# Bisection rounds 18 to 20 without prompt heads, the roots of the recurrence one round later, products without use on TensorE

## The reference, cut to what matters

```python
idx, valid = select_topk(indexer_scores(qi, wi, ki_all), q_pos, k_pos, topk)   # sample tokens: 256 of 4097
p = jax.nn.softmax(jnp.where(valid, logits + bias, -jnp.inf)); out = p @ v     # prompt: 8 heads, 4 blocks of 128 queries
u = jnp.sqrt(-jnp.expm1(2.0 * log_a)) * (i * xc)                               # recurrence, 512 channels
hs = scan(h = a * h + u)
```

## Time and profile before

| | us |
|---|---|
| median of the runs | 1295.65 |
| the profiled execution's own time | 1298.16 |
| its span, first to last instruction | 1296.4 |
| the stretch of the rounds in it | 210.0 to 283.4 |
| busy: PE, DVE, ACT, POOL | 1259.2, 696.9, 464.3, 186.4 |
| mean granted clock of PE | 0.986 |

### The profile page before, as it was taken

The page is one execution under the profiler, slowest core; times in us unless marked ns, Lnnn a source line. Parts: engine busy times, 40 slices in busy tenths (PEclk is TensorE's granted clock), DMA queues, the critical chain, the costliest instruction groups (busy, mean ns, idle before and its releaser), DMA issues.

```text
span 1296.4 us, 24716 instructions
## 1 busy us (share of the span) xinstructions
PE 1259.2 (97%) x10122; PEld 1219.1 (94%) x10122; DVE 696.9 (54%) x1292; ACT 464.3 (36%) x538; POOL 186.4 (14%) x281
## 2 busy tenths in 40 slices
PE   5999998899999999999999999999999999999997
PEld 5979995678999999999999999999999999999996
DVE  5468887677265555555323355547655555542222
ACT  5242326652153434334222244334433334331110
POOL 1101002135041111111000010034111111110000
PEclk9999989899999999999999999999999999999997
DMA  6653302023032222222222231222222222222211
GB/s 221 167 123 136 125 34 80 1 78 122 1 136 98 70 92 97 97 97 85 87 98 92 106 130 66 73 92 68 96 97 97 97 83 79 97 89 91 90 63 66
DMA packets 26595, 120.40 MB, mean 93 GB/s; under 512 B 7880, under 2 KB 9224, under 8 KB 14504
## 3 DMA queue, kind: packets, MB, share of 16 engines
q1 hardware_dynamic: 21784, 107.67, 24.4%
q0 software_dynamic: 2048, 10.54, 2.4%
q10 hardware_dynamic: 2704, 1.35, 0.4%
HBM read 115.94 MB, written 3.61 MB: 92 GB/s over the span
## 4 chain that ended last, share of the span: by engine, by line
PE 70%; DVE 2%; ACT 0%; issue 0%; DVEq 0%
PE ps L881 22%; PE ps L880 22%; PE ps L883 22%; PE ps L1016 1%; PE ps L1013 1%; PE ps L1014 1%; PE ps L899 1%; PE ps L1367 1%; DVE vtc L2028 0%; DVE yt L2075 0%; PE ps L1384 0%; DVE xn L1424 0%; PE ps L1397 0%; PE ps L1357 0%; DVE w_l L1410 0%; DVE ut L2021 0%
## 5 line engine op out<-in xcount | busy, mean ns | idle before, releaser
L880 PE MATMUL ps<-xh,w_h 128*128 128x260 f32 x1664 | 435.6, 283 | 0.2
L881 PE MATMUL ps<-xl,w_h 128*128 128x260 f32 x1664 | 434.7, 283 | 0.0
L883 PE MATMUL ps<-xh,w_l 128*128 128x260 f32 x1664 | 334.6, 283 | 0.0
L880 PEld LDWEIGHTS ps<-xh,w_h 128*128 128x128 f32 x1664 | 313.9, 189 | 0.7 <-DVE res L1829 0.3
L881 PEld LDWEIGHTS ps<-xl,w_h 128*128 128x128 f32 x1664 | 313.5, 188 | 0.1
L1410 DVE TENSOR_TENSOR w_l<-w_raw,w_h 128x2048 fp32r<-128x2048 f32 (+1 forms) x94 | 213.1, 2267 | 158.8 <-ACT w_h L526 158.6
L883 PEld LDWEIGHTS ps<-xh,w_l 128*128 128x128 f32 x1664 | 256.3, 188 | 0.0
L526 ACT ACTIVATE w_h<-w_raw 128x2048 fp32r<-128x2048 f32 (+1 forms) x50 | 92.3, 1846 | 256.4 <-PE ps L883 209.2
L881 PE MATMUL ps<-hl,w_h 128*128 128x260 f32 x704 | 184.0, 283 | 0.0
L880 PE MATMUL ps<-hh,w_h 128*128 128x260 f32 x704 | 183.5, 283 | 0.0
L883 PE MATMUL ps<-hh,w_l 128*128 128x260 f32 x704 | 142.0, 283 | 0.0
(11 more groups left out here) (325 smaller groups left out, 1569.9 us busy)
## 6 DMA issues: line engine op xcount, KB each, us to landing
w_raw<-in_wstream SPq DMA_DIRECT2D x86, 1024.0 KB, 4.8
w_raw<-in_wstream SPq DMA_DIRECT2D x8, 768.0 KB, 4.2
res<-in_x_t SPq DMA_DIRECT2D x4, 520.0 KB, 7.3
out_y<-yt SPq DMA_DIRECT2D x8, 260.0 KB, 2.2
tab<-bias_by_distance SPq DMA_DIRECT2D x16, 128.0 KB
wor<-in_wstream SPq DMA_DIRECT2D x4, 512.0 KB, 5.8
wm<-in_sgu_w ACTq DMA_DIRECT2D x1, 512.0 KB, 3.8
sb_b<-in_sgu_b ACTq DMA_DIRECT2D x1, 512.0 KB, 4.4
```

The costliest lines, as they stand in the source:

```text
L880: pe.matmul(out[h], wh, hi[h], start=(first and k == 0), stop=False)
L881: pe.matmul(out[h], wh, lo[h], start=False, stop=False)
L883: ins = pe.matmul(out[h], wl, hi[h], start=False, stop=(last and k == nk - 1))
```

## The change

`ROUND` loses its entries for rounds 18 to 20. Head 16 stays in round 17, heads 17 to 22 go two to a round into rounds 21 to 23, heads 23 to 31 keep rounds 24 to 32. With the table move the pairs on PE (heads 18 and 19 from round 18 to 20, heads 20 and 21 from round 20 to 21, heads 22 and 23 stay in round 22), the turns, the values and the copies. `roots` goes from ACT's round 17 to its round 18. In rounds 18 to 20 PE makes three products without use in PSUM bank 0, between `count` and `p_work`. What hangs on the last head of a block (`LAST`: head 15 in round 16, head 23 in round 24) stays in its round.

```diff
-        for rnd in range(17, 33):
+        ROUND[17] = (16,)
+        for rnd in range(21, 24):
+            ROUND[rnd] = (17 + 2 * (rnd - 21), 18 + 2 * (rnd - 21))
+        for rnd in range(24, 33):
             ROUND[rnd] = (rnd - 1,)
...
-                if rnd == 17:
+                if rnd == 18:
                     roots()
...
+            def warm_in(bank, k):
+
+                for n in range(k):
+                    pe.matmul(ps[:, bank, :], sameb[:], pickb[NCH - 1][:], start=True, stop=True)
...
                 if rnd < 9:
                     warm(3)
+                if 18 <= rnd < 21:
+                    pe.wait_ge(lg_done, 16)
+                    warm_in(0, 3)
                 p_work(rnd)
```

## The result

The kernel with the change takes 1308.33 us (median of four runs, 1306.06 to 1308.48) against 1295.49 us (1295.28 to 1296.06): ratio 1.0092 (taken over all runs; that of the two medians is 1.0099), 95% interval 1.008 to 1.0104. Forecast were 1299.0 us and a range up to 1301.3. The direction held, the size did not.

The account below looks back on a forecast made before the run. The rounds were taken as bound by their chains and what follows by PE; +1.7 to head 23's logits and +1.65 to the last logits made +3.35 on 1295.65, so 1299.0 us, range 1296.4 to 1301.3.

Parts of the forecast that it names:

- The chain of the forecast up to the scan: Rounds 18 to 21: the root waits for head 16's copy, then POOL, then the first scan at 254.3, +1.5 us.
- rounds 21 to 24: First scan to head 23's logits: two-head rounds through PE, partly at low clock, +0.8 to +2.2, taken +1.7 us.
- rounds 24 to 31: Head 23's logits to the last logits: one turn and two values more on PE, +1.65 us, between nothing and 3.
- The roots: ACT, round 18: root behind head 16's copy, which waits for its turn; root at 247.2, scan +1.5 us.
- the fifth rival: ACT pauses between table load and root, at most 1.28 us; scan at 255.6, total 1300.3 to 1302; chance 0.08.
- DVE and PE: Ahead of the first scan: DVE stands still 5.5 us waiting for POOL, PE idles 5.7 us from 250.25 to 255.95.
- with a low clock once more: Upper bound for head 23's logits to the last logits: all the extra PE work plus another low clock, 3 us.
- the backlog: PE work brought behind head 23's logits: one turn of 0.33 and two values of 0.65 each, +1.65 us.
- The claim of rows 2: Behind the last logits nothing can take up a delay: a microsecond won or lost there is one at the end.
- the backlog was not taken up: Rival: extra PE work fits into the tail's idle time and the clock returns early, 1296.8 to 1298.1; chance 0.17.
- The products: Rival, rounds 18 to 20: products without use do nothing, scan comes no later, 1295.7 to 1296.5; chance 0.06.
- The faster case: Rival: PE's clock stays at 2.4 GHz, last logits 2.7 to 3.5 us earlier, 1292.2 to 1293.0; chance 0.08.

Follow-up runs that it names:

- the later scans: The change with its four scans in rounds 23 to 26 instead of 21 to 24 and the sample step in 27: 1297.98 us, ratio 1.0014.
- the clock held: The change with products without use in PE's pauses, 26 in round 21 and 6 each in rounds 22 and 23: 1300.62 us, ratio 1.0036.
- the copies first: The change with ACT's copies of turned heads ahead of its exps in rounds 22 to 24: 1306.19 us, ratio 1.0086.
- 26 products ahead: The change with 26 further products without use on PE in round 21, between count and pair: 1306.18 us, ratio 1.0085.
- the table alone: The change with roots back in ACT's round 17 and no products without use in rounds 18 to 20: 1302.26 us, ratio 1.0045.
- the scans later at a held clock: The change with scans in rounds 23 to 26 and products without use (2, 6, 6) in rounds 21 to 23: 1295.73 us, ratio 0.9998.

## Why the prediction was wrong

The chain of the forecast up to the scan is there, step by step. The terms behind it were too small: "rounds 21 to 24", taken at +1.7 and measured at +3.6, and "rounds 24 to 31", taken at +1.65 and measured at +5.5. In both the low clock was priced too low, by the 7 us that it lasted before.

1. **The roots.** Forecast: root 3.5 us behind comparison 18, scan 1.5 us later than before. Measured 4.0 and 2.0. I had let the copy of head 16 wait for its turn alone. It also waits until the values of head 14 have read the buffer, and these stand behind the turn; the bracket at 244.08 names L1089, the values.
2. **The pause between load and root** (the fifth rival) is not there: the load starts at 244.59, the root at 245.88. The drain that the Trainium skill adds to each switch (ScalarE: Activation LUTs, What ACT_TABLE_LOAD costs) is not seen in this trace either. The table for exp was free, as I had it: it loads at 249.26, with 4.16 us of waiting behind it.
3. **DVE and PE.** DVE waits 5.97 us (5.5 forecast) and PE 6.11 (5.7). Comparison 22 came 0.2 us earlier than before instead of 0.7. That this wait is a cause, and not only beside one, the later scans show: 10.4 us by the medians, 6.7 in the rounds, with what they take off the low clock.
4. **Rounds 21 to 24: the step that failed first**, "+0.8 to +2.2, taken +1.7", measured +3.6. I took a low clock for the first pairs and turns, by the 7 us of before. But before, the 7 us were full of work (7.33 of 7.40 us), and here PE is busy 13.4 of 15.5 us, with pauses for logits and for ACT. With the clock held the logits of head 23 come at 264.65, 22.5 us behind comparison 18 and 2.2 later than before. So 1.4 of the 3.6 us is the clock, and at full clock 2.2 stand against my 0.8. Of these 1.4 us the later scan is 0.5 (step 1). I had also left out a second wait of the same kind, the turn of head 19 for the copy of head 17, which stands on ACT behind two exps: 1.32 us of PE's time at 263.54. That it costs time at the end is not shown: with the copies first the rounds were as long, and with the clock held it is 0.27 us.
5. **Rounds 24 to 31**: +1.65 forecast, 3 as the bound "with a low clock once more", measured +5.5. The low clock lasted until 270, into rounds 24 and 25, where the backlog of the two-head rounds lies (twelve values in 2.66 us). With the clock held the difference is +2.3 (20.9 us from 264.65 to 285.57), so the backlog was sized well enough and 3.2 us are the clock.
6. **The size of it**: holding the clock gives back 4.6 of 9.1 us in the rounds. The forecast had 3.35 for everything, and 0.9 of it for the clock (1.7 less the 0.8 at full clock). Of the 5.75 us that the rounds took more than forecast, 3.7 are the clock (0.5 in step 4, 3.2 in step 5), 1.4 the rounds 21 to 24 at full clock, and 0.65 the backlog. The other 3.7 us between +9.1 and the medians' +12.8 have no place in any trace. What was right is the structure; what was wrong is to price a clock by how long it was low elsewhere. The claim of rows 2 held: the last logits came 7.3 us later in the traces and the end 7.9.

Of the rivals, the backlog was not taken up. The products were indeed without clear effect (0.8 us by the medians and 0.6 of the other sign in the rounds), but the scan came later all the same, since ACT did wait for the copy of head 16. The faster case fell with the pause of 6.1 us. Its mechanism (the clock held at 2.4 GHz) is real, though: the kernel before gains 2.4 us by it.

## What to carry to other kernels

Moving work out of the rounds beside a slow operation gains nothing if the next instruction in the program of the same engine waits for that operation's result: follow the result to its first waiter, and move the waiter as well. Products without use belong into the pause itself, and before they are put anywhere, the trace says where the pause is; in a chain that has pauses of over a microsecond the clock can stay low long after the pause that brought it down (17 us here). Before a loss is put down to the clock, hold the clock in the kernel before as well: here that took the clock's part from 4.6 us to 1.9. Two units of work to a round need a look at every two-deep buffer, as each wait for "the one two before" becomes a wait within the round.

## What was not expected of the hardware

- A clock of 0.50 stayed for over 15 us in which PE was busy 13.4 of 15.5 us, and for 7 us where it was busy without a break. With 26 products ahead it still fell, 5 us behind them and 1.3 us behind a pause of 1.48 us.
- It falls without a pause too. In every trace it is at 0.50 once more behind the rounds, from between 344 and 359 us on, while PE is busy all the time (10.00 of 10.00 us at 0.51 from 359 in the change). In the 9 us before that fall PE had no pause either; 58 of its 83 products there have only 8 columns. What brings the fall about was not tried.
- Executions of one kernel differ by 2 to 3 us, and those of the kernel before by up to 5 (1293.28 to 1298.28). The low clock behind the rounds lasts 6.8 us (before, and the clock held), 10.2 or 13.7; from the last logits to the end the traces take 1012.0 to 1013.8, 1014.3 to 1015.7 and 1016.0 to 1016.5 us in this order. In the stage ahead of the rounds the clock of before is below 1.00 between 170 and 190 us (0.92 and 0.73 for ten microseconds each), as in the change (0.91 and 0.75). In the runs with the table alone and with the scans later at a held clock it is 1.00 there, and comparison 0 starts at 205.2 and 204.9 instead of 209.1 and 207.3. The 1.8 us between the last two are not the clock, which is low for 6.8 us in both; just ahead of the rounds DVE waits for a load of the scores there. What decides how long these low clocks last was not tried.
